# The first two projection blocks read x times the norm's weights, channel-major, and the inverse root is applied to their output

## The reference

```python
def rms_norm(x, gain):
    xf = x.astype(jnp.float32)
    inv = lax.rsqrt(jnp.mean(xf * xf, axis=-1, keepdims=True) + NORM_EPS)
    return (xf * inv).astype(x.dtype) * gain

h = rms_norm(x, attn_norm[l])
proj = h @ w_in[l]
q_r, k_r, v_r, g_r, q_m, k_m, v_m = jnp.split(proj, offsets, axis=-1)
...
gates = jax.nn.sigmoid(h @ w_gate[l] + b_gate[l])
```

## Time and profile before

| what | value |
|---|---|
| median of three runs | 488.93 us (488.80 to 488.98) |
| the profiled execution: span | 486.9 us |
| PE busy | 475.4 us (98%) |
| DVE busy | 296.1 us (61%) |
| ACT busy | 249.0 us (51%) |
| bytes moved by transfers | 86.65 MB, mean 178 GB/s |
| mean granted TensorE clock | 0.993 |

### The profile page before, as it was taken

How to read it: one execution, slowest core, us unless ns; L and a number is a source line. 1 busy time by engine, 2 the same in 40 slices (tenths; PEclk the granted TensorE clock), 3 DMA queues, 4 the chain that set the end, 5 groups by cost and what they waited for, 6 DMA issues and landing times.

```text
span 486.9 us, 7961 instructions
## 1 busy us (share of the span) xinstructions
PE 475.4 (98%) x3183; PEld 439.7 (90%) x3183; DVE 296.1 (61%) x354; ACT 249.0 (51%) x354; POOL 17.1 (4%) x26
## 2 busy tenths in 40 slices
PE   6999999999999999999999989999999999999997
PEld 4789999888888999999999868999999999988885
DVE  3854884574665546355337856488888777886312
ACT  3735332345884739333444625566666666673310
POOL 1000000311110001000000010000000000000000
PEclk9999999999999999999999997999999999999999
DMA  8996255144455524843453562144545555539002
GB/s 314 355 346 256 104 199 224 48 139 166 168 172 187 219 114 142 333 168 133 165 195 131 194 228 105 69 172 172 176 181 187 194 194 192 189 132 363 3 1 86
DMA packets 13400, 86.65 MB, mean 178 GB/s; under 512 B 1472, under 2 KB 1856, under 8 KB 3648
## 3 DMA queue, kind: packets, MB, share of 16 engines
q1 hardware_dynamic: 12096, 82.84, 45.7%
q10 hardware_dynamic: 864, 1.88, 1.1%
q0 software_dynamic: 416, 1.57, 0.9%
HBM read 85.24 MB, written 1.05 MB: 177 GB/s over the span
## 4 chain that ended last, share of the span: by engine, by line
PE 95%; DMA 1%; DVE 1%; ACT 1%; issue 0%; POOL 0%; POOLq 0%; SPq 0%
PE bank L333 18%; PE bank L334 18%; PE bank L335 18%; PE bank L293 7%; PE bank L295 7%; PE bank L294 7%; PE bank L526 4%; PE bank L523 4%; PE bank L524 4%; PE bank L350 2%; DMA xs<-x_dram 1%; PE bank L429 1%; PE bank L411 1%; PE bank L430 0%; PE bank L410 0%
## 5 line engine op out<-in xcount | busy, mean ns | idle before, releaser
L775 DVE TENSOR_TENSOR w_lo<-w_raw,w_hi 128x2048 fp32r<-128x2048 f32 x75 | 170.3, 2288 | 79.5 <-ACT w_hi L548 79.4
L333 PE MATMUL bank<-h_hi,w_hi 128*128 128x256 f32 x608 | 173.5, 285 | 0.7 <-DVE h_lo L980 0.7
L334 PE MATMUL bank<-h_lo,w_hi 128*128 128x256 f32 x608 | 172.7, 284 | 0.0
L335 PE MATMUL bank<-h_hi,w_lo 128*128 128x256 f32 x608 | 172.7, 284 | 0.0
L548 ACT ACTIVATE w_hi<-w_raw 128x2048 fp32r<-128x2048 f32 x75 | 141.6, 1915 | 33.4 <-PE bank L526 16.9
L333 PEld LDWEIGHTS bank<-h_hi,w_hi 128*128 128x128 f32 x608 | 117.5, 193 | 1.2 <-issue 1.1
L334 PEld LDWEIGHTS bank<-h_lo,w_hi 128*128 128x128 f32 x608 | 117.5, 193 | 0.1
L335 PEld LDWEIGHTS bank<-h_hi,w_lo 128*128 128x128 f32 x608 | 117.4, 193 | 0.0
L293 PE MATMUL bank<-w_hi,h_hi 128*128 128x512 f32 x160 | 63.1, 395 | 0.3 <-DVE w_lo L780 0.2
L295 PE MATMUL bank<-w_hi,h_lo 128*128 128x512 f32 x160 | 62.4, 390 | 0.0
L294 PE MATMUL bank<-w_lo,h_hi 128*128 128x512 f32 x160 | 62.3, 389 | 0.0
(11 more groups left out here) (112 smaller groups left out, 435.4 us busy)
## 6 DMA issues: line engine op xcount, KB each, us to landing
w_raw<-weights_dram SPq DMA_DIRECT2D x76, 1024.0 KB, 4.9
xs<-x_dram SPq DMA_DIRECT2D x2, 512.0 KB, 5.2
w_raw<-weights_dram SPq DMA_DIRECT2D x2, 512.0 KB, 8.3
xs<-x_dram POOLq DMA_DIRECT2D x1, 1024.0 KB, 7.9
out_dram<-ys SPq DMA_DIRECT2D x4, 256.0 KB, 2.0
area<-decay_dram ACTq DMA_DIRECT2D x1, 768.0 KB, 4.1
area<-gain_rows_dram ACTq DMA_DIRECT2D x1, 512.0 KB, 7.0
area<-gain_rows_dram POOLq DMA_DIRECT2D x1, 512.0 KB, 10.7
```

Source lines behind the costliest of these rows:

```text
L333: mm(o, s_hi, r_hi[:, k, :], start=(k == 0 and m % 2 == 0), stop=False)
L334: mm(o, s_hi, r_lo[:, k, :], start=False, stop=False)
L335: ins = mm(o, s_lo, r_hi[:, k, :], start=False, stop=(k == KT - 1 and m % 2 == 1))
L775: tt(w_lo[r][:, :], raw[r][:, :], w_hi[r][:, :].bitcast(f32), ALU.subtract).then_inc(lo_ready, 1)
```

## The change

It does five things.

1. **Second copy of x.** The host also hands over x channel-major (`x_chan`, 128 partitions x 8 tiles of 256 tokens, 1 MB). SP loads it in three parts (256, 256 and 512 KB) between the two parts of w0 and ahead of w1. The token-major x is now loaded behind w2 and ahead of w3, to ys.
2. **Operands of V_R0 and V_R1.** For each of the 8 channel tiles k, ACT writes xg_hi = x_t * gain (an Identity activation with a per-partition scale) and DVE writes xg_lo = x_t * gain - xg_hi. These alternate with the quarters of w0 and w1. No transposes are needed. The norm's weights come as a 128 x 8 tile instead of a 512 KB broadcast row.
3. **Inverse root.** ACT squares token tile 0 between split(2) and split(3), DVE squares tile 1 there as well. The root scales v_r as ACT evicts it (`scale_block` for `copy_block`).
4. **h for all later blocks.** PE turns the root into a row over all partitions with two 128 x 128 products behind the first half of V_R1 (`inv_rows`). DVE then writes hn_t = x_t * gain * inv in 8 instructions of 256 elements, ACT makes h_hi of it in two of 1024, DVE h_lo in two of 1024. On both engines this is second[V_R0], so it stands between split(4) and split(5). Q_R waits for `h_ready`.
5. **Warm-up.** 8 matmuls instead of 17 and 6.

```diff
-WARM_UP = 17, 6
+WARM_UP = 8
@@ sync
-            for t in range(NT):
-                sp.dma_start(x_tok[:, t, :], x_view[:, t, :]).then_inc(x_loaded[t], 16)
             for c in range(2):
+                load_x_chan(c, 2 * c, 2 * c + 2)
                 part = slice(c * HALF_ELEMS // 2, (c + 1) * HALF_ELEMS // 2)
                 sp.dma_start(raw[0][:, part], weights[0, :, part]).then_inc(raw_loaded[0] if c else raw_start, 16)
+            load_x_chan(2, 4, KT)
             for r in range(1, SLOTS):
                 sp.dma_start(raw[r][:, :], weights[r]).then_inc(raw_loaded[r], 16)
+                if r == 2:
+                    for t in range(NT):
+                        sp.dma_start(y_tok[:, t, :], x_view[:, t, :]).then_inc(x_loaded[t], 16)
@@ tensor, token_block
+                        pe.wait_ge(xg_lo_ready, 4 * h + kk + 1)
...
+                    if b == V_R1 and h == 0:
+                        inv_rows()
@@ tensor, channel_block
+                    if b == Q_R:
+                        pe.wait_ge(h_ready, h + 1)
@@ tensor
-            keep_warm(WARM_UP[0])
+            keep_warm(WARM_UP).then_inc(warm_done, 1)
+            def inv_rows():
+                pe.wait_ge(ident_loaded, 16)
+                pe.wait_ge(inv_x_ready, NT)
+                o = start_unit("inv_row", 0)
+                for t in range(NT):
+                    ins = mm(o[:, P * t:P * t + P], inv_x[:, t:t + 1].broadcast_to([P, P]), ident[:, :],
+                             start=(t == 0), stop=(t == NT - 1))
+                ins.then_inc(unit_made, 1)
...
-            h_transposes(0)
-            keep_warm(WARM_UP[1])
-            token_block(V_R0)
-            token_block(V_R1)
+            token_block(V_R0, (xg_hi, xg_lo))
+            token_block(V_R1, (xg_hi, xg_lo))
@@ scalar
+            act.dma_start(gain_col[:, :], gain_cols).then_inc(gain_col_loaded, 16)
             act.dma_start(ident[:, :], ident_in).then_inc(ident_loaded, 16)
-            act.dma_start(gain_row, gain_rows[0:1, :].partition_broadcast(P)).then_inc(gain_loaded, 16)
+            def xg_high(k):
+                A(xg_hi[:, k, :], x_t[:, k, :], ACT.Identity, scale=gain_col[:, k:k + 1]).then_inc(xg_hi_ready, 1)
+            act.wait_ge(gain_col_loaded, 16)
+            for k in range(KT):
+                if k in (0, 2, 4):
+                    act.wait_ge(x_chan_loaded[k // 2], 16)
+                xg_high(k)
+                split_quarter(k // 4, k % 4)
             act.dma_start(rotary, rotary_in).then_inc(rotary_loaded, 16)
             act.dma_start(decay, decay_in).then_inc(tables_loaded, 16)
             act.dma_start(mask[:, :], mask_in).then_inc(tables_loaded, 16)
             act.dma_start(col[:, :], cols).then_inc(tables_loaded, 16)
+            split(2)
+            act.wait_ge(x_loaded[0], 16)
+            A(square_out, y_tok[:, 0, :], ACT.Square, accum_out=ss_x[:, 0:1]).then_inc(sums_x[0], 1)
+            split(3)
             act.wait_ge(tables_loaded, 48)
+            for t in range(NT):
+                act.wait_ge(inv_x_ready, t + 1)
+            def h_high():
+                for kh in range(2):
+                    k = slice(4 * kh, 4 * kh + 4)
+                    if kh == 0:
+                        act.wait_ge(hn_ready, 1)
+                    else:
+                        wait_unit_read(act, unit("inv_row", 0))
+                    A(h_hi[:, k, :], hn_t[:, k, :], ACT.Copy).then_inc(h_hi_ready, 1)
@@ vector
+            def normalise():
+                u = unit("inv_row", 0)
+                dve.wait_ge(unit_made, u + 1)
+                for k in range(KT):
+                    ins = stt(out=hn_t[:, k, :], in0=x_t[:, k, :], scalar=gain_col[:, k:k + 1], in1=ubank(u)[:, 0:SEQ],
+                              op0=ALU.mult, op1=ALU.mult)
+                    if k == 3:
+                        ins.then_inc(hn_ready, 1)
+                ins.then_inc(unit_read[u % 4], 1)
+                for kh in range(2):
+                    k = slice(4 * kh, 4 * kh + 4)
+                    dve.wait_ge(h_hi_ready, kh + 1)
+                    tt(h_lo[:, k, :], hn_t[:, k, :], h_hi[:, k, :].bitcast(f32), ALU.subtract).then_inc(h_ready, 1)
```

More of the change, by code:

```diff
@@ L50, with hybrid_layer @@
 COLS = COL_CONV + CONV_COLS
-def hybrid_layer(nc, x, weights, gain_rows, cols, ident_in, mask_in, rotary_in, decay_in, out):
+def hybrid_layer(nc, x, x_chan, weights, gain_row_in, gain_cols, cols, ident_in, mask_in, rotary_in, decay_in, out):
     f32 = mybir.dt.float32
@@ L134, in hybrid_layer @@
         raw_start = sem("raw_start")
+        x_chan_loaded = [sem(f"x_chan_loaded{c}") for c in range(3)]
+        gain_col_loaded = sem("gain_col_loaded")
+        xg_hi_ready = sem("xg_hi_ready")
+        xg_lo_ready = sem("xg_lo_ready")
+        hn_ready = sem("hn_ready")
+        warm_done = sem("warm_done")
         hi_ready = sem("hi_ready")
@@ L279, in start_unit, with token_half @@
                 return ubank(u)
-            def token_half(out_banks, n, tiles, first, last, order=None, chunk0=None, before=None):
+            def token_half(out_banks, n, tiles, first, last, order=None, chunk0=None, before=None, src=(h_hi, h_lo)):
                 hi = w_hi[n % SLOTS][:, :].rearrange("p (k c) -> p k c", k=4)
@@ L289, in token_half @@
                     k = tiles[kk]
-                    s_hi = h_hi[:, k, P * t:P * t + P]
-                    s_lo = h_lo[:, k, P * t:P * t + P]
+                    s_hi, s_lo = (part[:, k, P * t:P * t + P] for part in src)
                     o = out_banks[t][:, :]
@@ L298, in token_half, with token_block @@
                 return ins
-            def token_block(b):
+            def token_block(b, src=(h_hi, h_lo)):
                 for h in range(2):
@@ L311, in quarter_split @@
                             pe.wait_ge(lo_ready, n + 1)
[L313 to L316, removed]
+                    if b > 0:
                         pe.wait_ge(lo_ready, n + 1)
@@ L361, in keep_warm @@
                 for _ in range(count):
-                    mm(bank[7][:, :], w_lo[SLOTS - 1][:, 0:P], w_lo[SLOTS - 1][:, 0:512], start=True, stop=True)
-            keep_warm(WARM_UP[0])
-            pe.wait_ge(ident_loaded, 16)
-            def h_transposes(kh):
+                    ins = mm(bank[7][:, :], w_lo[SLOTS - 1][:, 0:P], w_lo[SLOTS - 1][:, 0:512], start=True, stop=True)
+                return ins
+            keep_warm(WARM_UP).then_inc(warm_done, 1)
[3 more added lines that the diff above has]
+                o = start_unit("inv_row", 0)
                 for t in range(NT):
-                    pe.wait_ge(xn_ready, 2 * kh + t + 1)
-                    transposes("h", 2 * kh + t, [y_tok[:, t, P * k:P * k + P] for k in range(4 * kh, 4 * kh + 4)])
+                    ins = mm(o[:, P * t:P * t + P], inv_x[:, t:t + 1].broadcast_to([P, P]), ident[:, :],
+                             start=(t == 0), stop=(t == NT - 1))
+                ins.then_inc(unit_made, 1)
             def tail_ret_scores():
@@ L686, in _ @@
             first = {
[L687 to L688 removed]
+                V_R0: lambda: scale_block(V_R0, lambda t: v_r[:, t, 0:512]),
+                V_R1: lambda: scale_block(V_R1, lambda t: v_r[:, t, 512:1024]),
                 G_R0: lambda: silu_gates(G_R0), G_R1: lambda: silu_gates(G_R1),
@@ L705, in _ @@
             second = {
+                V_R0: h_high,
                 Q_M1: lambda: ret_read(0), K_M0: lambda: ret_read(1),
@@ L801, in _ @@
+            nc.vector.memset(w_lo[SLOTS - 1][:, 0:512].bitcast(f32), 0.0).then_inc(zeros_ready, 1)
+            dve.wait_ge(gain_col_loaded, 16)
+            for k in range(KT):
+                if k in (0, 2, 4):
+                    dve.wait_ge(x_chan_loaded[k // 2], 16)
+                xg_low(k)
+                split_quarter(k // 4, k % 4)
+            split(2)
             dve.wait_ge(x_loaded[1], 16)
-            nc.vector.tensor_tensor_reduce(out=y_tok[:, 1, :], in0=x_tok[:, 1, :], in1=x_tok[:, 1, :], scale=1.0,
+            nc.vector.tensor_tensor_reduce(out=square_out2, in0=y_tok[:, 1, :], in1=y_tok[:, 1, :], scale=1.0,
@@ L812, in _ @@
-            for n in range(2, SLOTS):
-                split(n)
+            dve.wait_ge(warm_done, 1)
+            split(3)
             dve.wait_ge(rotary_loaded, 16)
@@ L994, in _ @@
             second = {
+                V_R0: normalise,
                 G_R1: group_norm,
```

70 lines of the change are left out of this document (23 added, 47 removed).

## The result

| | before | after |
|---|---|---|
| median of 12 runs | 487.94 us (486.56 to 490.20) | 491.76 us (490.31 to 492.90) |
| ratio | | 1.0074, 95% interval 1.0057 to 1.0092 |
| span of the profiled execution | 486.9 us | 489.9 us |
| mean granted clock | 0.993 | 0.986 |

The forecast was 488.3, with a range up to 490.3. The two profiled executions are 3.0 us apart, the medians 3.8.

The account below looks back on a forecast made before the run. PE was taken to bound the kernel, with DMA near its limit. Of 7 us won, stalls (0.7, 0.9, 2.3, 2.3) and small terms take back 6; Q_R starts 1.05 earlier, 0.65 kept: 488.3, range 486.6 to 490.3.

Parts of the forecast that it names:

- First real matmul: At the head, V_R0's first matmul was to start at 6.9 instead of 13.20.
- The eight products: DVE's eight scalar_tensor_tensor of 256 that make h ahead of Q_R, say 3.4 us.
- the two h_lo: DVE's h_lo instructions of 1024 elements, the last work ahead of Q_R, about 1.2 us each.
- The cold start: V_R0 starting after 8 zero matmuls instead of 17, claimed hidden by the 3 us of stalls behind it.
- V_R1's end: PE alone was to be through V_R1 at 33.1, split and matmuls after w3 has landed.
- w3's landing: Transfer for V_R1's second half: 22.4 to 24.5, taken as 23.4, with all four tables' 1.29 MB counted ahead.
- V_R0 ended: V_R0 was to end at 18.5 instead of 25.55, after a stall of 0.7 for w1.
- The clock falls in a stall: Rival, chance 0.17: the clock falls in PE's stall ahead of Q_R, 1.8 to 3.4 us lost, time 490.3.
- The feed is late: Rival, chance 0.20: w3 lands at 25 or more, Q_R at 37.0 or later, time 489.5.
- From w3 to Q_R: Split, evictions and making of h between w3's landing and Q_R: 12.0 us, Q_R at 35.4 after a 2.3 stall.
- The second norm: Clock returns there at a fixed place or with the matmuls, so 0.65 of the 1.05 us gain was taken.

Follow-up runs that it names:

- e1: The changed kernel with the waits for the rotary, decay, mask and column tables moved to their first use; ratio 0.9903 to the kernel before.
- e2: The changed kernel with the four table loads issued by SP behind the token-major x instead of by ACT; ratio 0.9923 to the kernel before.
- f1: e1 with 17 zero matmuls at the start instead of 8; ratio 0.9895 to the kernel before.
- f4: The changed kernel with the four tables in two loads of longer rows, same queue and bytes; ratio 0.9917 to the kernel before.
- e3: The kernel before with 32 bytes per partition left free ahead of h_hi; ratio 0.9930 to the kernel before.
- f3: e1 with 17 zero matmuls and the tables issued by ACT behind split(4); ratio 0.9875 to the kernel before.
- f2: The changed kernel with 32 matmuls of no use between V_R1 and Q_R; ratio 1.0039 to the kernel before.
- g2: f3 with 6, 3 and 2 matmuls of no use in PE's three waits of the second norm; ratio 0.9828 to the kernel before, 480.12 us.

## Why the prediction was wrong

**Right.** First real matmul 7.49 (6.9). The chain from w3 to Q_R, which e1 shows without the wait for the tables: 12.2 us (12.0), 0.55 of it a wait for w4. The eight products took 3.22 (3.4), the two h_lo 2.43 (2.4). The cold start was hidden.

**Right in part by luck.** V_R1's end, 33.2 (33.1), and w3's landing, 22.7 (22.4 to 24.5, taken 23.4). V_R0 ended at 21.5 and not at 18.5, since it ran at half pace at first; that went into the stalls ahead of w1, w2 and w3. Even at full pace (e1) it ended at 20.7: PE waited 0.8 us for the second part of w0, which no term has, and w1 landed at 12.9 or later (11.7). And w3 landed in the forecast range with only rotary and a part of decay landed ahead of it, where all four tables were counted. "The clock falls in a stall" came true, at 1.7 us, but in a stall of 7.4 and not in the forecast one of 2.3: where the stall ahead of Q_R was 1.4 to 1.9 us (e1, e2, f1, f4), the clock stayed at 1.00 through it.

**The step that failed** is "From w3 to Q_R". It starts ACT's two scaled evictions as soon as w3 is split, at L3 + 1.95, and puts the wait for the tables, which stands ahead of them in the program on ACT and again on DVE, at nothing without a reason. It was 6.18 us. The tables entered the sum only under "w3's landing", as bytes ahead of w3, and it was never asked when they land themselves. In the kernel before the wait cost nothing: the cols table, issued at 18.41, landed 6.0 later, at 24.4, and ACT's first eviction was due only at 25.83.

```profile
18.41 0.45 ACTq L579 DMA_DIRECT2D col<-cols_dram  x1
...
25.83 1.09 ACT L587 ACTIVATE area<-bank 128x512 f32<-128x512 f32 x2 [1.89 <-PE bank L295]
```

```profile
col<-cols_dram ACTq DMA_DIRECT2D x1, 105.0 KB, 6.0
```

In the changed kernel it was issued at 14.24 and landed at 30.8, while ACT was ready to evict at 24.65. So the wait grew by 6.4 us because the table came later and by 1.2 because ACT came earlier, less the 1.4 us of slack. It was issued earlier and came later, beside a full queue of SP's. Before, the DMA engines had a pause at 17 to 19, as SP issued w4 only at 18.76. Rotary's own delay, 6.9 us for 256 KB beside a full queue, was a clue. An estimate by turns of one row: with 128 rows a load spread over 16 DMA engines, the 32 table rows of each engine have 32 rows of the weights beside them. With the tables' own bytes that is 5.5 MB, 13 us at 416 GB/s, of the 17.9 us from the first issue to the last landing; f4's two loads make 3.4 MB, 8 us of its 12.5. The 4 to 5 us left over in both are not explained.

**The missing term** made PE's stall 7.4 instead of 2.3, and the clock fell in it. "The feed is late" was not it: w3 was early.

**The unseen gain.** PE's pace by placement, -0.7% (e3). No step of the prediction looked at where gain_col lies. Without it the time would have been near 495.

**The second norm.** "The three runs lie within 0.18, which speaks for a return at a fixed place" does not stand: 12 runs of the same kernel spread by 3.6 us. The return is not at a fixed place either, it moves with the matmuls: up-projection from 295.30 and return at 298.9 before, 292.35 and 295.9 in e1, 300.10 and 303.7 in the changed kernel. So the 0.4 us taken off for it were not due. And among the profiled executions some show the fall there (before, the changed kernel, e1, f3) and some don't (e3, f1, f2), with the same code in that place.

## What to carry to other kernels

When a change makes an engine arrive earlier, list every wait that the others pass on the way to it, those that cost nothing today too, and give each its own landing time; put a wait at the first use of what it waits for. A table in short rows on a second queue, beside a full queue of long rows, lands by its number of rows or loads and not by its bytes: join such tables, or put them in the stream's queue. Before a change is credited or blamed for 1%, check PE's pace in code that it leaves alone: a new tile ahead of the operands can be worth nearly as much, and two executions with the same placement can differ by a quarter of a per cent in it.

## What the runs showed of the hardware

- Moving h and a by 32 bytes a partition changed the start-to-start distance of 256-column matmuls that stream them from 0.120 to 0.117 us and that of 512-column matmuls that load them from 0.227 to 0.233. Moves of 32 and 64 bytes did nearly the same. Between 0.117 and 0.118 the pace also changed with the placement left alone, 1.2 us over an up-projection (f1, g2).
- With loads queued deep, the core took 416 GB/s for 14 us. The Trainium skill ("DMA: Bandwidth & Descriptors", Specifications) gives some 358 GB/s as the limit of HBM for a core, which it gets as half of what two cores share; this trace, of a kernel on one core, does not agree with it as a limit.
- The clock fell at 37.5 in an idle stretch that began at 33.2, and at the second norm in some executions and not in others, with the same code there; with three bursts of fillers, 11 matmuls in all, it stayed up in all five runs (g2).
